# Sample attention: both latent halves' products with a stream's new keys on separate rows of the array, and key tiles shared between two units

## What is computed

```python
# per stream b: 512 cached latent rows and 16 new ones, 528 keys; 16 heads, 16 new queries
ckv_all = jnp.concatenate([past_ckv, ckv_new], axis=1)          # (8, 528, 256)
k_nope, v = mla_expand(ckv_all, w_kv_b, k_norm)                 # v = ckv_all @ w_v, per head
s = (einsum('bqhd,bkhd->bhqk', q_nope, k_nope) + einsum('bqhr,bkr->bhqk', q_rope, k_rope)) * ATTN_SCALE
p = softmax(s, axis=-1)
o = einsum('bhqk,bkhd->bqhd', p, v)
```

## Time and profile before

| | |
|---|---|
| median of 3 executions | 1838.68 us (1837.64 to 1839.15) |
| the profiled execution | 1838.27 us |
| its span | 1836.5 us |
| PE busy | 1807.6 us, 98% of the span |
| DVE busy | 1135.9 us, 62% |
| ACT busy | 828.1 us, 45% |
| granted TensorE clock | 9 (of at most 9) in all 40 slices |
| the chain that ended last | PE 85%, DVE 9%, ACT 3%, issue 2%, DMA 1% |
| sample part, units 0 to 15 | about 1400 to 1477 us of the span |

### The profile page before, as it was taken

One profiled execution on the slowest core, in us unless ns is written; L12 is line 12 of the kernel. 1 busy time (PEld: TensorE's weight loads), 2 busy tenths in 40 slices (PEclk: granted clock), 3 DMA queues, 4 the chain that ended last, 5 costly groups with the idle time before them and its releaser, 6 DMA issues.

```text
span 1836.5 us, 28276 instructions
## 1 busy us (share of the span) xinstructions
PE 1807.6 (98%) x10567; PEld 1732.0 (94%) x10567; DVE 1135.9 (62%) x1706; ACT 828.1 (45%) x1420; POOL 228.6 (12%) x280
## 2 busy tenths in 40 slices
PE   9999999999999999999999999999998999999998
PEld 9999999799888999999999999996777999999998
DVE  6454447879889645444775454456778856454445
ACT  6333336665564433333553333346665544333333
POOL 1000110311311000011400001122112131000110
PEclk9999999999999999999999999999999999999999
DMA  6434444456352544454344444451124534444442
GB/s 212 137 116 135 138 138 154 151 207 235 122 206 87 193 125 127 125 150 137 116 142 120 134 117 139 139 171 40 47 82 138 173 116 128 133 121 130 143 138 76
DMA packets 68452, 249.48 MB, mean 136 GB/s; under 512 B 8264, under 2 KB 10568, under 8 KB 67088
## 3 DMA queue, kind: packets, MB, share of 16 engines
q1 hardware_dynamic: 58880, 206.86, 37.1%
q0 software_dynamic: 9488, 41.48, 6.6%
HBM read 235.51 MB, written 12.12 MB: 135 GB/s over the span
## 4 chain that ended last, share of the span: by engine, by line
PE 85%; DVE 9%; ACT 3%; issue 2%; DMA 1%; POOL 0%; DVEq 0%; ACTq 0%; POOLq 0%
PE pair L1913 24%; PE pair L1914 24%; PE pair L1915 24%; DVE wlo L1245 2%; PE pair L2422 2%; PE pair L2331 2%; PE pair L2333 2%; PE pair L2332 2%; DVE cy L1372 1%; DVE S L1468 1%; PE pair L1920 0%; PE pair L1922 0%; PE pair L1921 0%; PE pair L2121 0%; DVE xsT L1475 0%
## 5 line engine op out<-in xcount | busy, mean ns | idle before, releaser
L1913 PE MATMUL pair<-xh,whi 128*128 128x384 f32 x1960 | 660.2, 337 | 2.4 <-DVE xl L1255 1.5
L1915 PE MATMUL pair<-xh,wlo 128*128 128x384 f32 x1960 | 654.9, 334 | 0.0
L1914 PE MATMUL pair<-xl,whi 128*128 128x384 f32 x1960 | 654.8, 334 | 0.0
L1245 DVE TENSOR_TENSOR wlo<-raw,whi 128x1024 fp32r<-128x1024 f32 (+3 forms) x371 | 464.2, 1253 | 160.2 <-ACT whi L708 159.4
L708 ACT ACTIVATE whi<-raw 128x1024 fp32r<-128x1024 f32 (+2 forms) x369 | 378.1, 1028 | 261.7 <-PE pair L1915 257.7
L1913 PEld LDWEIGHTS pair<-xh,whi 128*128 128x128 f32 x1960 | 367.9, 188 | 9.3 <-DVE wlo L1245 3.8
L1914 PEld LDWEIGHTS pair<-xl,whi 128*128 128x128 f32 x1960 | 368.0, 188 | 1.6 <-issue 1.0
L1915 PEld LDWEIGHTS pair<-xh,wlo 128*128 128x128 f32 x1960 | 367.9, 188 | 0.0
L1265 DVE TENSOR_TENSOR tg<-pair,rstd 128x384 f32<-128x384 f32 x88 | 49.1, 557 | 326.1 <-PE pair L1915 325.4
L1913 PE MATMUL pair<-ah,whi 128*128 128x384 f32 x704 | 235.2, 334 | 0.0
L1914 PE MATMUL pair<-al,whi 128*128 128x384 f32 x704 | 235.1, 334 | 0.0
(11 more groups left out here) (408 smaller groups left out, 2198.3 us busy)
## 6 DMA issues: line engine op xcount, KB each, us to landing
raw<-in_stream SPq DMA_DIRECT2D x372, 512.0 KB, 3.7
S<-in_ssm POOLq DMA_DIRECT2D x4, 2048.0 KB, 9.1
out_ssm_s<-S POOLq DMA_DIRECT2D x4, 2048.0 KB, 7.8
seg<-acs_rows POOLq DMA_DIRECT2D x12, 512.0 KB, 5.9
cTb<-in_cacheT POOLq DMA_DIRECT2D x10, 512.0 KB, 4.2
kn<-rs_rows SPq DMA_DIRECT2D x16, 264.0 KB
lowC<-in_cache SPq DMA_DIRECT2D x8, 512.0 KB, 3.2
lowA<-in_cacheT POOLq DMA_DIRECT2D x6, 512.0 KB, 5.1
```

What stands on the lines that cost most here:

```text
L1245: V.tensor_tensor(wlo[:, r, 0:w], raw[:, r, 0:w], whi[:, r, 0:w].bitcast(F32), ALU.subtract).then_inc(lo_ready, 1)
L1913: M(out, whi[:, r, ws], mh_(k), start=first and k == k0, stop=False)
L1914: M(out, whi[:, r, ws], ml_(k), start=False, stop=False)
L1915: ins = M(out, wlo[:, r, ws], mh_(k), start=False, stop=last and k == k1 - 1)
```

## The change

The 16 new rows of a stream are loaded twice, to partitions 0 to 15 and 32 to 47 of `vnew` (one more transfer of 16 x 256 per stream, and the counts waited for grow from 32 to 48). VectorE writes the scaled probabilities of the 16 new keys a second time, 16 columns on, so that the fifth transposed tile has them on partitions 0 to 15 and 32 to 47; this is one more `tensor_scalar` of 128 x 16 per unit, in a `step`. For streams 1 to 6 the even unit's call does key tiles 0 and 1 of both halves and the odd unit's call tiles 2 and 3 of both, and then the new keys of half 0 on rows 0 to 31 and of half 1 on rows 32 to 63 of the array. For streams 0 and 7 the halves stay apart, with 32 rows for the new keys. ScalarE copies both halves out in the odd units.

```diff
             def past_values(b):
...
-                sp.dma_start(vnew[0:STEPS, b % 2, :], ckv[STEPS * b:STEPS * b + STEPS, 2, :]).then_inc(cn_ld[b % 2], 16)
+                for at in (0, 32):
+                    sp.dma_start(vnew[at:at + STEPS, b % 2, :], ckv[STEPS * b:STEPS * b + STEPS, 2, :]).then_inc(cn_ld[b % 2], 16)
...
-            pool.wait_ge(cn_ld[1], 32 * 4)
+            pool.wait_ge(cn_ld[1], 48 * 4)
...
             for u in range(UNITS):
                 if u % 2 and u // 2 + 2 < STREAMS:
                     keys_split(u // 2 + 2)
-                if u >= 2:
+                if u >= 3 and u % 2:
+                    s_latent(u - 3)
                     s_latent(u - 2)
...
                 step(V.reciprocal(sm[:, o + 5:o + 6], sm[:, o + 4:o + 5]))
+                step(V.tensor_scalar(Pb[:, s, KEYS + STEPS:KEYS + 2 * STEPS], Pb[:, s, PAST:KEYS], sm[:, o + 5:o + 6], None, ALU.mult))
                 V.tensor_scalar(Pb[:, s, 0:KEYS], Pb[:, s, 0:KEYS], sm[:, o + 5:o + 6], None, ALU.mult).then_inc(p_ready, 1)
...
             def s_values(n):
-                b, c = divmod(n, 2)
-                pe.wait_ge(pt_ev, MH + 2 * b + 2)
-                pe.wait_ge(cn_ld[b % 2], 32 * (b // 2 + 1))
-                if b:
-                    pe.wait_ge(s_out_kept, n - 1)
-                for j in range(5):
-                    v = cnat[:, b % 2, j, tiles(c)] if j < 4 else vnew[:, b % 2, tiles(c)]
-                    ins = M(bank[1 if c else 7][:, 0:256], v, PTs[:, b % 2, j, :], start=j == 0, stop=j == 4)
-                ins.then_inc(po_ps, 1)
+                b, second = divmod(n, 2)
+                if not second:
+                    pe.wait_ge(pt_ev, MH + 2 * b + 2)
+                    pe.wait_ge(cn_ld[b % 2], 48 * (b // 2 + 1))
+                    if b:
+                        pe.wait_ge(s_out_kept, 2 * b)
+                if b in (0, STREAMS - 1):
+                    for j in range(4):
+                        M(bank[1 if second else 7][:, 0:256], cnat[:, b % 2, j, tiles(second)], PTs[:, b % 2, j, :],
+                          start=j == 0, stop=False)
+                    M(bank[1 if second else 7][:, 0:256], vnew[0:32, b % 2, tiles(second)], PTs[0:32, b % 2, 4, :],
+                      start=False, stop=True).then_inc(po_ps, 1)
+                    return
+                for j in (2, 3) if second else (0, 1):
+                    for c in range(2):
+                        M(bank[1 if c else 7][:, 0:256], cnat[:, b % 2, j, tiles(c)], PTs[:, b % 2, j, :],
+                          start=j == 0, stop=False)
+                if second:
+                    for c in range(2):
+                        new = slice(32 * c, 32 * c + 32)
+                        ins = M(bank[1 if c else 7][:, 0:256], vnew[new, b % 2, tiles(c)], PTs[new, b % 2, 4, :],
+                                start=False, stop=True)
+                    ins.then_inc(po_ps, 2)
```

## The result

The changed kernel takes 1841.82 us (median of 22 executions, 1840.56 to 1844.76), the kernel before 1839.20 us (median of 22, 1837.62 to 1840.99) beside it. The ratio is 1.0016 with a 95% interval of 1.0010 to 1.0022: 2.6 us slower, inside the 0.2% that was called no change, but clear of zero. The forecast was + 1.8 us and no change; the time lies in the range.

What follows compares the result with a forecast made beforehand. A ring of VectorE and ScalarE, not TensorE, was taken to bound the sample part. 1.21 us up to the last transposes plus 0.62 behind them, about + 1.8 on 1838.68, gave 1840.5 us, range 1837.0 to 1842.6.

Steps and rivals of the forecast that it cites:

- The ring of VectorE and ScalarE: Sample part: VectorE's 8.5 us of work and two waits for ScalarE set the 9.04 us cycle per stream.
- what TensorE saves: Streams 1 to 6: 0.43 us saved in the even unit becomes a wait for VectorE, booked at 0.
- Rival A: TensorE owns the cycle: 1836.1 us with free switching, 1839.2 with 0.31 per visit to narrow tiles; chance 0.15.
- the pair: Odd unit's new-key products of both halves: two slots of 0.216 us, and up to 0.31 for switching tiles.
- Rivals B and C: Halves' products overlap partly: three slots, 1841.6, chance 0.09; or not at all: four slots, 1843.1, chance 0.08.
- The end: Stream 7's two calls, each ending with a lone 32-row product on the chain: 0.31 us each, 0.62 together.
- a switch that reaches the ring: Upper end for odd units: 0.06 us per stream of tile switching delays the ring, five times, 0.3 in all.
- VectorE's second copy: One more VectorE operation per unit: 0.21 us, hidden in even units, uncovered in odd ones, period 9.04 to 9.25.
- what the end gives back: Unit 15: waits of 0.25 us before its maximum and 0.69 before its transposes absorb 0.94 of 2.15.
- the start: Units 0 to 3, not yet in step: 0.42 us, then 0.26 from the latent copies, together 0.68 slower.
- the two copies of the latents: ScalarE's copies before the odd unit's exponential: hidden with 0.25 us in hand, booked at 0.
- The norms: Key norms on SyncE's queue: put off 0.65 us by the extra load, more than 5 us in hand, costing nothing.

Runs made afterwards that it cites:

- e2: The kernel before with only VectorE's second copy of the 16 probabilities added: 1840.92 us, ratio 1.0011 to the kernel before.
- e4: The kernel before with the fifth product of every call on 32 rows instead of 128: 1843.20 us, ratio 1.0020 to the kernel before.
- e9: The kernel before with SyncE asking for the next unit's key norms ahead of the cached rows: 1839.31 us, ratio 1.0000.
- e10: The changed kernel with SyncE asking for the key norms ahead of the cached rows: 1842.11 us, ratio 1.0013 to the kernel before.
- e6: The changed kernel with one operation writing both probability copies and stream 7's new keys as a pair too: 1840.73 us, ratio 1.0008 to the kernel before.
- e12: As e6, with SyncE asking for the key norms first: 1840.07 us, ratio 1.0004 to the kernel before.
- e11: As e7, with SyncE asking for the key norms first: 1839.25 us, ratio 1.0000 to the kernel before.
- e8: The changed kernel without VectorE's low part of the cached latent keys for streams 3 to 7: 1843.11 us, ratio 1.0020 to the kernel before.
- e7: The kernel before without VectorE's low part of the cached latent keys for streams 3 to 7: 1841.37 us, ratio 1.0012.
- e1: The changed kernel without VectorE's second copy of the 16 probabilities: 1840.62 us, ratio 1.0012 to the kernel before.

## Why the prediction was right, and where it was off

**Right: who owns the cycle.** The ring of VectorE and ScalarE sets the time, and what TensorE saves becomes a wait for VectorE, 0.35 us ahead of the scores of each even unit. e2 is the proof: the copy alone, TensorE's program untouched, gives the period of the changed kernel. Rival A falls with it, though it was close: TensorE's own cycle, as estimated from e4, is 8.91 against the ring's 9.04.

**Right: the pair.** Two slots for four records, and 0.29 a visit where I had taken up to 0.31 from the scan. Rivals B and C fall: e4's two lone records take the same 0.63. So does the reading of program order by which three slots would be needed. The end, 0.62 forecast for two lone narrow products on the chain, measured 0.64.

The forecast and the measured time, slice by slice (starts of the reciprocals of units 0, 5, 13 and 15, of the transposes of unit 15, of the first head product):

| slice | forecast | measured |
|---|---|---|
| unit 0 to unit 5 | 0.68 | 0.43 |
| unit 5 to unit 13 | 4 x 0.21 = 0.84 | 37.54 - 36.17 = 1.37 |
| unit 13 to unit 15 | 0.42 - 0.25 = 0.17 | 8.44 - 8.13 = 0.31 |
| unit 15 to its transposes | 0.21 - 0.69 = -0.48 | -0.13 |
| on to the first head product | 0.62 | 0.64 |
| sum | 1.83 | 2.62 |

The measured 2.6 is above what the terms of the forecast allowed, 1.8 and 0.3 for a switch that reaches the ring. (By these terms the upper end of the forecast's own range is 1838.68 + 2.1 = 1840.8, not 1841.3.) The time lies in the range that was given because that had been widened to cover rivals A and B. The last transposes come 1.98 us later against the start of the part, not 1.2.

**Mis-sized: VectorE's second copy.** I took 0.21 us, near the reciprocal's 0.20; it is 0.27 (the operation itself runs 0.23, the reciprocal 0.16). In the odd unit it is uncovered. In the even unit I took the 0.24 of idle time for its cover. Directly behind the scaling L1835 starts 0.52 after it (1441.14 - 1440.62), before it started 0.73 after (1439.21 - 1438.48): 0.21 of cover, and 0.06 come through. 0.27 + 0.06 is the period's 0.34 but for rounding, where I had 0.21. This is the largest part of the miss, 0.53 from unit 5 to unit 13, and 0.12 of the 0.14 up to unit 15.

**Mis-sized: what the end gives back.** I booked 0.69 for the time that the scaling of unit 15 had in hand. TensorE in the changed kernel there:

```profile
1472.97 0.70 PE L2438 MATMUL pair<-lowA,ckv 32*128 32x256 f32 x4
1473.60 0.77 PE L2468 MATMUL pair<-ident,Pb 128*128 128x128 f32 x5
```

It goes from the pair to the transposes of unit 15 without idle time: the transposes stand behind TensorE's own work, as before, and this now has the visit of 0.29 in it. From the first score product of unit 15 to the transposes it takes 6.60 us instead of 6.78, so TensorE saves 0.18 there, where I had counted 0.43. I had written that its path there was the same within 0.3, and this 0.3 is the error, 0.35 of the miss.

**Not measured: the start.** The slice came out 0.25 below the forecast, but one pair of profiles can't size it: e9 and e10, the same two kernels but for the order of SyncE's queue, have 25.47 and 26.26, 0.79 apart instead of 0.43. Two things vary there from profile to profile: a wait of VectorE for the scores of unit 1 or 2 (1.05 us in e6 and e12, 0.93 in e11, none before and after), and when the load lands that ScalarE waits for in unit 3 (2.04 before, 1.73 after, 1.41 in e2, 2.25 in e8). I had put this wait off by as much as everything else; whether that is right stays open.

**Argued wrongly, without effect: what is in the ring.** I wrote that all of VectorE's 8.5 us were in it. e7 shows that 1.1 of them are not. And the two copies of the latents, booked at nothing as hidden with 0.25 in hand, are hidden only behind the second copy: e1 uncovers 0.22 per stream. I had compared their end with an exponential already put off by 0.21.

**SyncE.** The norms, said to have more than 5 us, were never late in the profiles of the changed kernel, and e10 gains nothing. But the margin is thinner than I claimed: in e7 they were asked for at 1438.48 and VectorE waited for them until 1445.67. So a load took up to 7.2 us there, where the kernel before needs it some 6 after its issue at 1437.63.

## What to carry to other kernels

When several engines go in step, look for the ring of waits that sets the cycle, which need not pass through the busiest of them, and price a change by what it puts on that ring: here 0.27 us of VectorE outweighed 0.43 us of TensorE, because TensorE was not in it. Two small delays side by side cost only the longer one, so taking one away shows the other, and each has to be measured alone. Here products side by side on separate rows shared their time in full, but each visit to narrow tiles cost 0.29 us, and results that ended together were also copied out together, behind the last product.

## What was not expected of the hardware

- A visit to 32-row tiles between 128-row ones costs 0.29 us here, whether for one f32 product or for two side by side; the weight loads don't run ahead over the switch.
- A VectorE operation on 16 columns that the next one waits for holds it back by 0.27 us; one on 32 columns that nothing waits for, by 0.16.
- Less work for VectorE made a kernel 2.2 us slower (e7; 0.6 to 3.9 by its interval), with waits for late norms of 0.90 and 1.09 us, and another order of one queue took that back (e11).
